# The first sixteen taps of one depthwise-conv tile move to GpSimd, and VectorE's table of filler steps is written anew

## The chip, the cores and the metric

The kernel runs on one core of a Trainium2 chip. The metric is the device time of one execution in microseconds (us); the median of three is compared. In the text PE is TensorE, DVE is VectorE, ACT is ScalarE, POOL is GpSimd, and SP is the engine that issues the DMAs.

## The reference, cut to what matters

One decoder layer over 512 positions of width 1024:

```python
h = rms_norm(x, norm_mix_g)
ca, cg, q, k, v, iq, ik, iw, z, xbc, dt = jnp.split(h @ w_in, SPLITS, axis=-1)
u = ca * jax.nn.sigmoid(cg)                  # 512 channels
u = causal_dwconv(u, conv_dw_w, conv_dw_b)   # 31 taps along the positions
u = jax.nn.silu(layer_norm(u, conv_ln_g, conv_ln_b))
att = sparse_attention(qh, kh, vh, iq, ik, iw, rel_bias)   # each query keeps its top 128 keys
y = ...                                      # Mamba-2 scan of xbc, gated by z, normed
x = x + jnp.concatenate([u, att, y], axis=-1) @ w_out
h = rms_norm(x, norm_ffn_g)
fa, fg = jnp.split(causal_dwconv(h @ w_up, ffn_conv_w, ffn_conv_b), 2, axis=-1)
x = x + (jax.nn.silu(fg) * fa) @ w_down
```

The change is about two steps. The depthwise convolution with 31 taps works on four tiles of 128 channels by 512 positions, and each tap adds a shifted copy of `u`, times one weight per channel, to a running sum. The top 128 keys are found by 16 rounds for each of three blocks of 128 queries (the first block needs none); a round takes the eight largest scores of each row and then marks them as taken.

## The kernel before, in words

All products are in split single precision: each weight chunk of 512 columns by 512 rows (or the same amount in another shape) is rounded to a high part on ACT (`w_hi`, L934), DVE subtracts it from the original for the low part (`w_lo`, L640), and PE multiplies three times. The mixing part of the layer has 23 chunks, each done in four quarters. A quarter is a slot: slot n is quarter n mod 4 of chunk n // 4, and it holds 12 matmuls of 512 columns. After its quarter, PE does small pieces of the other branches (indexer products, transposes, attention scores and so on).

One list, `PLAN`, holds all steps of the mixing part in one order, slot by slot. Every engine walks through the same list and issues its own share in that order, with semaphores between engines, so an instruction that waits holds up all that stand behind it on its engine. Within a slot come first the `front` steps (such as `logit` and `share` of the attention softmax), then the slot's matmuls and small pieces, and then the `fill` steps. The low part of chunk c is a fill step of slot 4c - 3; the high part, of slot 4c - 4.

The fill steps of DVE's long streams are set by a table, `FILL`: for each slot a string in which `1`, `2`, `3` is the next step of the top-k stream of query block 1, 2 or 3 (take the eight largest, L1357; mark them, L1362; 16 times, then the selection mask, L1367) and `a`, `d` the next tap of conv tile 0 or 3. A tap on DVE is one instruction with two SBUF inputs, `u_acc<-u_in,prm,u_acc` (L622; the first is a product alone, L617). Block 1 has 256 scores in a row, block 2 has 384, block 3 has 512.

Conv tiles 1 and 2 are on POOL, in slots that `POOL_SLOTS` names. POOL's tap is an addition of two SBUF inputs (L860); the product before it is made by ACT (`dwp`, L1129), two slots ahead, into one of four buffers named `tapped`. Product i waits until tap i - 4 is done, because it reuses its buffer. ACT stands in line behind that wait with everything else that it has: rounding the weights, evacuating the PSUM banks of q, k, v and of the indexer (`iqT` L927, `relu` L1010), the exponentials (L1052, L1060) and the evacuation of transposed probabilities (L1070).

POOL also computes the inverse roots of the q and k norms (L840), in slots 17 to 20 and 25 to 28.

An attention unit u (16 in all: four query blocks by four pairs of heads) has `score` on PE, `logit` on DVE in the next slot (L1406, which adds the bias and takes the row's minimum), the exponential on ACT, then in the slot after it the reciprocal on DVE (L1412) and the scaling on ACT (L1060), then the transpose on PE (L1773), its evacuation on ACT (L1070) and the product with v (L1975). Scores, transposes and the small products share a ring of three PSUM banks: PE can start the next one only when the bank of three before has been emptied.

The chunks are: conv 0 (slots 0 to 3), indexer (4 to 7), conv 1 (8 to 11), q, k, v (12 to 35), conv 2 and 3 (36 to 43), the scan's inputs (44 to 67), the output projection (68 to 91). After that come the feed-forward chunks, which the change does not touch.

The functions that the diff touches:

Of the kernel before, what the change touches and what calls it, by code (L numbers as in the profile page):

```python
# [20 lines left out]
CONV_CH, CONV_K = 512, 31  # L21
# [42 lines left out]
def bucket_onehot():  # L64
# [10 lines left out]

FILL = {6: "aa", 7: "aaa", 8: "aaa", 10: "1121", 11: "1212", 12: "31213", 14: "2131", 
# [4 lines left out]
        48: "ddadd", 50: "da", 51: "dd", 52: "dadd", 54: "dad", 55: "d", 56: "addda", 58: "ddd",   # L81
        59: "dd", 60: "dddd", 62: "ddd"}
POOL_SLOTS = {1: {15: 1, 16: 2, 21: 2, 22: 1, 23: 2, 24: 2, 29: 2, 30: 2, 31: 1, 32: 2, 33: 2,
# [7 lines left out]
SSD_SLOTS = (68, 72, 76, 80)  # L91
DW_POOL = (1, 2)


# [9 lines left out]
def make_plan():  # L104
# [36 lines left out]
    for j in range(4):  # L141
        streams["abcd"[j]] = iter([("dw", j, i) for i in range(CONV_K)])

# [52 lines left out]
    for j, counts in POOL_SLOTS.items():  # L196
        at_ = [n for n, k in counts.items() for _ in range(k)]
        for i, n in enumerate(at_):
            fill[n].append(("dw", j, i))
            if i:  # L200
                fill[n - 2].append(("dwp", j, i))
    for n, letters in FILL.items():
# [169 lines left out]
def build(nc, x, rel_bias, norm_mix_g, w_in, conv_dw_w, conv_dw_b, conv_ln_g, conv_ln_b, q_norm_g,  # L372
# [7 lines left out]
    with ExitStack() as ctx:  # L380
# [4 lines left out]
        def at(name, shape, dt, offset=None):  # L385

            size = (int(np.prod(shape[1:])) * (2 if dt == BF16 else 4) + 31) // 32 * 32
            if offset is None:
                offset = top[0]
                top[0] += size  # L390
            return nc.alloc_sbuf_tensor_at(name, shape, dt, offset=offset)

        def region(kb):
# [71 lines left out]
        tapped = {1: at("tapped1", [P, 4, 512], F32, r6 + 8 * K),  # L465
                  2: at("tapped2", [P, 4, 512], F32, r1)}
        gssm = at("gssm", [P, 512], F32)
        dec = at("dec", [P, SH, P], F32, rs)
# [347 lines left out]
        def _(pool):  # L816
# [25 lines left out]
            for s in PLAN:  # L842
# [5 lines left out]
                elif k == "qkms":  # L848
                    i = NT * "qk".index(s[1]) + s[2]
                    pool.wait_ge(qkms_ready, i + 1)  # L850
                    inverse_root(rqk[:, NH * i:NH * i + NH], ssqk[:, NH * i:NH * i + NH], rqk_ready)
                elif k == "dw" and s[1] in DW_POOL:

                    _, j, i = s
                    if i == 0:
                        tap(pool, j, i)
                    else:
                        pool.wait_ge(dw_taps[j], i)
                        pool.wait_ge(dwp_ready, DW_POOL.index(j) * (CONV_K - 1) + i)
                        pool.tensor_tensor(u_acc[:, j, i:], tapped[j][:, i % 4, 0:SEQ - i],  # L860
                                           u_acc[:, j, i:], ALU.add).then_inc(dw_taps[j], 1)
# [50 lines left out]
        def _(act):  # L912
# [36 lines left out]
            for s in PLAN:  # L949
# [171 lines left out]
                elif k == "dwp":  # L1121
# [3 lines left out]
                    if i > 4:  # L1125
                        act.wait_ge(dw_taps[j], i - 3)
                    elif i == 1:
                        act.wait_ge(glu_ready, j + 1)
                    act.activation(tapped[j][:, i % 4, 0:SEQ - i], u_in[:, j, 0:SEQ - i], ACT.Copy,  # L1129
                                   scale=prm[:, c:c + 1]).then_inc(dwp_ready, 1)  # L1130
# [112 lines left out]
        def _(dve):  # L1243
# [18 lines left out]
            for s in PLAN:  # L1262
# [63 lines left out]
                elif k == "glu":  # L1326
# [4 lines left out]
                        .then_inc(glu_ready, 1)  # L1331
                elif k == "dw" and s[1] not in DW_POOL:
                    tap(dve, *s[1:])
# [825 lines left out]
```

## Time and profile before

| what | value |
|---|---|
| median of 3 runs | 717.45 us (717.26 to 717.74) |
| the profiled execution's own time | 717.7 us |
| its span | 716.0 us |
| PE busy | 697.0 us, 97% of the span |
| DVE busy | 545.4 us, 76% |
| ACT busy | 380.6 us, 53% |
| POOL busy | 141.8 us, 20% |
| granted TensorE clock | 1.00 of full speed |

The profile is one execution. A row of the timeline has the start, the duration of the row, the engine, the line of the program, the operation, output and inputs, and xN for N instructions in one row; in brackets stands how long the engine had been idle before and what ended it. A PE matmul of 512 columns is shown as 0.39 us because matmuls overlap; one starts every 0.23 us.

### The profile page before, as it was taken

How to read it: one execution, taken by the hardware profiler on the slowest of the kernel's cores; microseconds unless marked ns; L12 is line 12 of the kernel's file. 1: busy time of each engine (PE TensorE's matmuls, PEld its weight loads, DVE VectorE, ACT ScalarE, POOL GpSimd, SP SyncE). 2: the span in 40 equal slices, each digit the busy share in tenths (PEclk: the TensorE clock that was granted, in tenths of full speed). 3: DMA queues.
4: the chain of work that ended last, by engine and by line, in shares of the span. 5: the costliest groups of instructions: out<-in, count | busy, mean ns of one | idle time of the engine just before them, and what ended most of it. 6: DMA issues, size and time to landing. Idle time of an engine off the chain costs nothing.

```text
span 716.0 us, 9787 instructions
## 1 busy us (share of the span) xinstructions
PE 697.0 (97%) x3402; PEld 560.4 (78%) x3402; DVE 545.4 (76%) x852; ACT 380.6 (53%) x570; POOL 141.8 (20%) x114
## 2 busy tenths in 40 slices
PE   4999999999999999999999999999999999999998
PEld 4776888667666788788888888888888888888886
DVE  4368989988898947667667777876766866997895
ACT  6254655988878765633464343343343343654660
POOL 2000477944564402233410000000000000000000
PEclk9999999999999999999999999999999999999999
DMA  8731314211111141312234588656687547864552
GB/s 245 235 127 60 118 59 117 62 60 59 59 60 60 59 177 61 135 70 60 59 118 140 173 246 249 190 170 200 186 249 237 179 160 298 297 221 140 169 162 88
DMA packets 87554, 104.09 MB, mean 145 GB/s; under 512 B 6871, under 2 KB 65591, under 8 KB 87519
## 3 DMA queue, kind: packets, MB, share of 16 engines
q1 hardware_dynamic: 87375, 103.12, 45.9%
q10 hardware_dynamic: 144, 0.52, 0.2%
q8 instruction: 20, 0.33, 0.2%
q14 instruction: 15, 0.12, 0.1%
HBM read 87.10 MB, written 16.54 MB: 145 GB/s over the span
## 4 chain that ended last, share of the span: by engine, by line
PE 87%; ACT 7%; DVE 4%; issue 2%; DMA 1%; POOL 0%; DVEq 0%; ACTq 0%
PE bank L1767 75%; PE bank L1773 4%; PE bank L1787 2%; ACT tapped L1129 1%; ACT w_hi L934 1%; PE bank L1975 1%; DVE u_acc L622 1%; PE bank L2031 1%; PE bank L1951 1%; DVE xbcT L1427 1%; PE bank L1926 1%; DMA x_in<-in_x 1%; ACT prob L1052 1%; ACT dec L1099 0%; DVE prob L1406 0%
## 5 line engine op out<-in xcount | busy, mean ns | idle before, releaser
L1767 PE MATMUL bank<-h_hi,w_hi 128*128 128x512 f32 (+1 forms) x496 | 192.9, 389 | 0.0
L1767 PE MATMUL bank<-h_lo,w_hi 128*128 128x512 f32 (+1 forms) x496 | 189.9, 383 | 0.0
L1767 PE MATMUL bank<-h_hi,w_lo 128*128 128x512 f32 (+1 forms) x496 | 189.8, 383 | 0.0
L1767 PEld LDWEIGHTS bank<-h_hi,w_hi 128*128 128x128 f32 x496 | 93.2, 188 | 25.7 <-issue 7.8
L1621 DVE SCALAR_TENSOR_TENSOR f<-bank,prm,f 128x511 f32<-128x511 f32 x88 | 65.8, 748 | 60.7 <-ACT f L1182 55.2
L1767 PEld LDWEIGHTS bank<-h_hi,w_lo 128*128 128x128 f32 x496 | 93.2, 188 | 18.4
L1767 PEld LDWEIGHTS bank<-h_lo,w_hi 128*128 128x128 f32 x496 | 93.3, 188 | 17.3
L860 POOL TENSOR_TENSOR u_acc<-tapped,u_acc 128x511 f32<-128x511 f32 (+29 forms) x60 | 90.1, 1502 | 46.1 <-ACT tapped L1129 43.0
L1182 ACT ACTIVATE f<-bank,prm 128x512 f32<-128x512 f32 x44 | 34.2, 777 | 70.4 <-PE bank L1767 70.2
L640 DVE TENSOR_TENSOR w_lo<-w_raw,w_hi 128x2048 fp32r<-128x2048 f32 x24 | 55.6, 2316 | 8.9 <-ACT w_hi L934 8.7
L1767 PE MATMUL bank<-w_hi,g_parts 128*128 128x512 f32 x168 | 53.8, 389 | 0.0
L1596 DVE TENSOR_TENSOR w_lo<-w_raw,w_hi 128x2048 fp32r<-128x2048 f32 x22 | 50.3, 2287 | 3.4 <-ACT w_hi L1171 3.4
L622 DVE SCALAR_TENSOR_TENSOR u_acc<-u_in,prm,u_acc 128x511 f32<-128x511 f32 (+29 forms) x60 | 51.9, 877 | 0.8
L1189 ACT ACTIVATE sg<-f 128x512 f32<-128x512 f32 x22 | 13.9, 632 | 72.4 <-DVE f L1621 72.4
L1129 ACT ACTIVATE tapped<-u_in,prm 128x511 f32<-128x511 f32 (+29 forms) x60 | 40.2, 704 | 21.4 <-POOL u_acc L860 15.5
L1767 PE MATMUL bank<-w_hi,h_hi 128*128 128x512 f32 x128 | 51.2, 400 | 0.0
L1767 PE MATMUL bank<-w_hi,h_lo 128*128 128x512 f32 x128 | 50.0, 390 | 0.0
L1767 PE MATMUL bank<-w_lo,h_hi 128*128 128x512 f32 x128 | 49.9, 390 | 0.0
L934 ACT ACTIVATE w_hi<-w_raw 128x2048 fp32r<-128x2048 f32 x24 | 45.8, 1910 | 3.5 <-DMA w_raw<-in_w_in 2.2
L840 POOL TENSOR_TENSOR stats<-stats 128x1 f32<-128x1 f32 (+1 forms) x24 | 23.1, 966 | 103.4 <-DVE stats L1507 35.1
L1171 ACT ACTIVATE w_hi<-w_raw 128x2048 fp32r<-128x2048 f32 x22 | 41.9, 1906 | 0.0
L1767 PEld LDWEIGHTS bank<-w_hi,g_parts 128*128 128x128 f32 x168 | 31.5, 188 | 6.6
(279 smaller groups left out, 1228.2 us busy)
## 6 DMA issues: line engine op xcount, KB each, us to landing
w_raw<-in_w_up SPq DMA_DIRECT2D x44, 512.0 KB, 6.1
w_raw<-in_w_in SPq DMA_DIRECT2D x34, 512.0 KB, 4.6
down_raw<-in_w_down SPq DMA_DIRECT2D x22, 512.0 KB, 5.4
weight_sums<-down_raw SPq DMA_DIRECT2D x11, 768.0 KB, 5.3
w_raw<-in_w_out SPq DMA_DIRECT2D x12, 512.0 KB, 4.5
weight_sums<-w_sum SPq DMA_DIRECT2D x11, 512.0 KB, 2.7
w_raw<-weight_sums SPq DMA_DIRECT2D x6, 768.0 KB, 6.0
down_raw<-weight_sums SPq DMA_DIRECT2D x5, 768.0 KB, 4.4
```

The source lines that it names most:

```text
L622: eng.scalar_tensor_tensor(out=u_acc[:, j, i:], in0=u_in[:, j, 0:SEQ - i], scalar=w, in1=u_acc[:, j, i:], op0=ALU.mult, op1=ALU.add).then_ ...
L640: eng.tensor_tensor(wlo[:, slot, cols], wraw[:, slot, cols], whi[:, slot, cols].bitcast(F32), ALU.subtract).then_inc(ready, 1)
L840: pool.tensor_tensor(out_, in_, half_neg[:, 0:n], ALU.pow).then_inc(ready, 1)
L860: pool.tensor_tensor(u_acc[:, j, i:], tapped[j][:, i % 4, 0:SEQ - i], u_acc[:, j, i:], ALU.add).then_inc(dw_taps[j], 1)
L934: act.activation(whi[:, c % NSLOT, :], wraw[:, c % NSLOT, :], ACT.Copy)\
L1129: act.activation(tapped[j][:, i % 4, 0:SEQ - i], u_in[:, j, 0:SEQ - i], ACT.Copy, scale=prm[:, c:c + 1]).then_inc(dwp_ready, 1)
L1171: act.activation(whi[:, c % NSLOT, :], wraw[:, c % NSLOT, :], ACT.Copy)\
L1182: act.activation(fbuf[:, 2 * s + v, :], bank[FFN_BANK[2 * s + v]][:, :], ACT.Identity, bias=prm[:, bass.ds(tile + R_FB, 1)], scale=prm[:, ...
L1596: dve.tensor_tensor(wlo[:, c % NSLOT, :], wraw[:, c % NSLOT, :], whi[:, c % NSLOT, :].bitcast(F32), ALU.subtract)\
L1621: ins = dve.scalar_tensor_tensor(out=fbuf[:, 2 * s + v, i:], in0=bank[FFN_BANK[2 * s + v]][:, 0:SEQ - i], scalar=prm[:, bass.ds(tile + (R_ ...
L1767: ins = pe.matmul(o, a, b, start=first and i == 0 and q == 0, stop=last and i == n - 1 and q == 2)
L1773: return pe.transpose(o, in_, ident[0:n, 0:n])
```

## The change

Tile 0's taps 0 to 15 go from DVE to POOL, in slots 6 to 14, with ACT making products 1 to 15 for them. Tile 0 shares the four `tapped` buffers of tile 1, so ACT's first product of tile 1 now waits until all 16 taps of tile 0 are done. Taps 16 to 30 of tile 0 stay on DVE, and the order of DVE's fill steps is another from slot 6 on. A product is no longer placed ahead of the slot in which its tile's first tap stands.

```diff
-FILL = {6: "aa", 7: "aaa", 8: "aaa", 10: "1121", 11: "1212", 12: "31213", 14: "2131", 
...
-        48: "ddadd", 50: "da", 51: "dd", 52: "dadd", 54: "dad", 55: "d", 56: "addda", 58: "ddd", 
-        59: "dd", 60: "dddd", 62: "ddd"}
-POOL_SLOTS = {1: {15: 1, 16: 2, 21: 2, 22: 1, 23: 2, 24: 2, 29: 2, 30: 2, 31: 1, 32: 2, 33: 2,
+FILL = {10: "11211", 11: "2121", 12: "32131", 14: "2132", 15: "12312", 16: "131a2", 18: "31", 
...
+        55: "d", 56: "dddd", 58: "ddd", 59: "d"}
+POOL_SLOTS = {0: {6: 1, 7: 2, 8: 2, 9: 2, 10: 2, 11: 2, 12: 2, 13: 1, 14: 2},
+              1: {15: 1, 16: 2, 21: 2, 22: 1, 23: 2, 24: 2, 29: 2, 30: 2, 31: 1, 32: 2, 33: 2,
...
+POOL0 = 16
+def on_pool(j, i):
+    return j in DW_POOL or (j == 0 and i < POOL0)
+def products_to(j, i):
+    return i if j == 0 else POOL0 - 1 + DW_POOL.index(j) * (CONV_K - 1) + i
...
-        streams["abcd"[j]] = iter([("dw", j, i) for i in range(CONV_K)])
+        streams["abcd"[j]] = iter([("dw", j, i) for i in range(CONV_K) if not on_pool(j, i)])
...
-                fill[n - 2].append(("dwp", j, i))
+                fill[max(n - 2, at_[0])].append(("dwp", j, i))
...
+        tapped[0] = tapped[1]
...
-                        pool.wait_ge(dwp_ready, DW_POOL.index(j) * (CONV_K - 1) + i)
+                        pool.wait_ge(dwp_ready, products_to(j, i))
...
                     elif i == 1:
                         act.wait_ge(glu_ready, j + 1)
+                        if j == DW_POOL[0]:
+                            act.wait_ge(dw_taps[0], POOL0)
```

The first place is ACT in slots 6 to 9, behind the evacuation of the first indexer tile. Before:

```order
L991 ACTIVATE u_acc<-u_acc 128x512
L927 ACTIVATE iqT<-bank 128x512 x2
L1010 ACTIVATE relu<-bank 128x256 x4
L934 ACTIVATE w_hi<-w_raw 128x2048
L1010 ACTIVATE relu<-bank 128x384 x4
```

and now:

```order
L939 ACTIVATE iqT<-bank 128x512
L1143 ACTIVATE tapped_103<-u_in,prm 128x511
L1143 ACTIVATE tapped_103<-u_in,prm 128x510
L1143 ACTIVATE tapped_103<-u_in,prm 128x509
L1143 ACTIVATE tapped_103<-u_in,prm 128x508
L1143 ACTIVATE tapped_103<-u_in,prm 128x507
L1143 ACTIVATE tapped_103<-u_in,prm 128x506
L939 ACTIVATE iqT<-bank 128x512
L1022 ACTIVATE relu<-bank 128x256 x4
L946 ACTIVATE w_hi<-w_raw 128x2048
```

Six products now stand between the evacuations of the two indexer tiles, and the last two of them wait for POOL's taps 1 and 2.

The second place is DVE from the low part of chunk 9 (slot 33) to the first `logit` (slot 35), which empties a bank of the first attention score. Before:

```order
L640 TENSOR_TENSOR w_lo<-w_raw,w_hi 128x2048
L1362 MATCH_REPLACE rank<-stats,rank 128x256
L1362 MATCH_REPLACE rank<-stats,rank 128x384
L1362 MATCH_REPLACE rank<-stats,rank 128x512
L1357 MAX stats<-rank 128x8 x2
L622 SCALAR_TENSOR_TENSOR u_acc<-u_in,prm,u_acc 128x498
L1406 ISA prob,stats<-bank,tbias 128x128
```

and now:

```order
L652 TENSOR_TENSOR w_lo<-w_raw,w_hi 128x2048
L1371 MAX stats<-rank 128x8 x2
L1376 MATCH_REPLACE rank<-stats,rank 128x512
L634 SCALAR_TENSOR_TENSOR u_acc<-u_in,prm,u_acc 128x491
L1376 MATCH_REPLACE rank<-stats,rank 128x256
L1376 MATCH_REPLACE rank<-stats,rank 128x384
L1371 MAX stats<-rank 128x8
L1420 ISA prob,stats<-bank,tbias 128x128
```

One more step, a search for the eight largest of 512, stands between the low part and the first `logit`.

The third place is DVE from the `logit` of unit 8 (slot 46) to that of unit 9 (slot 48); `att_lo` is the low part of query block 1's attention output, and behind it comes unit 8's reciprocal. Before:

```order
L617 TENSOR_SCALAR u_acc<-u_in,prm 128x512
L622 SCALAR_TENSOR_TENSOR u_acc<-u_in,prm,u_acc 128x511
L622 SCALAR_TENSOR_TENSOR u_acc<-u_in,prm,u_acc 128x510
L1418 TENSOR_TENSOR att_lo<-bank,att_hi 128x4x128
L1412 RECIPROCAL stats<-stats 128x2
```

and now:

```order
L629 TENSOR_SCALAR u_acc<-u_in,prm 128x512
L634 SCALAR_TENSOR_TENSOR u_acc<-u_in,prm,u_acc 128x511
L634 SCALAR_TENSOR_TENSOR u_acc<-u_in,prm,u_acc 128x510
L634 SCALAR_TENSOR_TENSOR u_acc<-u_in,prm,u_acc 128x509
L634 SCALAR_TENSOR_TENSOR u_acc<-u_in,prm,u_acc 128x508
L1432 TENSOR_TENSOR att_lo<-bank,att_hi 128x4x128
L1426 RECIPROCAL stats<-stats 128x2
```

Two taps more stand ahead of `att_lo` and of unit 8's reciprocal. In slots 47 to 51, that is from there to the `logit` of unit 11, there were 10 taps and are now 9.

## Rows read from the trace of the kernel before

**Rows 1.** The page: busy time of each engine.
```profile
PE 697.0 (97%) x3402; PEld 560.4 (78%) x3402; DVE 545.4 (76%) x852; ACT 380.6 (53%) x570; POOL 141.8 (20%) x114
```

**Rows 2.** Waits of PE: for whom, us in total, times, longest.
```profile
PE bank L1773 <- DVE x_normed L1274: 9.7, 1, 9.7
PE bank L1773 <- ACT dec L1099: 0.8, 2, 0.5
```

**Rows 3.** Timeline of PE: the six waits between 120 and 215 us.
```profile
128.76 0.63 PE L1773 MATMUL bank<-ident,k_tok 128*128 128x128 f32 x4 [0.80 <-ACT kT L1027]
...
136.84 0.23 PE L1947 MATMUL bank<-neg_q_bf,ident_bf 128*128 128x128 bf16 x1 [0.95 <-DVE stats L1406]
...
144.52 0.44 PE L1975 MATMUL bank<-probT,v_tok 128*64 128x128 f32 x4 [0.35 <-ACT probT L1070]
...
187.13 0.52 PE L1773 MATMUL bank<-ident,prob 128*128 128x128 f32 x3 [1.03 <-ACT prob L1060]
...
195.20 0.88 PE L1975 MATMUL bank<-probT,v_tok 128*64 128x128 f32 x12 [0.33 <-ACT probT L1070]
...
212.77 0.88 PE L1975 MATMUL bank<-probT,v_tok 128*64 128x128 f32 x12 [0.53 <-ACT probT L1070]
```

**Rows 4.** Timeline of DVE in slots 5 to 13, and its next long wait.
```profile
45.07 0.69 DVE L1330 TENSOR_TENSOR u_in<-u_in,u_acc 128x512 f32<-128x512 f32 x1 [1.27 <-ACT u_acc L991]
...
48.31 3.11 DVE L622 SCALAR_TENSOR_TENSOR u_acc<-u_in,prm,u_acc 128x511 f32<-128x511 f32 x4
...
65.38 1.61 DVE L1345 SCALAR_TENSOR_TENSOR rank<-relu,stats,rank 128x512 f32<-128x512 f32 x2 [1.02 <-ACT relu L1010]
...
71.57 2.28 DVE L640 TENSOR_TENSOR w_lo<-w_raw,w_hi 128x2048 fp32r<-128x2048 f32 x1
...
106.86 0.69 DVE L1374 TENSOR_REDUCE stats<-sq 128x8 f32<-128x512 f32 x1 [3.40 <-ACT sq L1021]
```

**Rows 5.** Timeline of PE: indexer pieces of slot 8; the first matmul of slot 16.
```profile
49.42 1.93 PE L1926 MATMUL bank<-ikT,iqT 64*128 64x256 f32 x8
...
75.68 0.39 PE L1767 MATMUL bank<-w_hi,h_hi 128*128 128x512 f32 x1
```

**Rows 6.** Timeline of ACT: indexer evacuation, first products of tile 1, a wait for POOL.
```profile
46.81 0.60 ACT L927 ACTIVATE iqT<-bank 128x512 f32<-128x512 f32 x1 [1.22 <-PE bank L1767]
50.16 0.66 ACT L1010 ACTIVATE relu<-bank 128x256 f32<-128x256 f32 x2 [2.75 <-PE bank L1926]
...
74.49 1.34 ACT L1129 ACTIVATE tapped<-u_in,prm 128x511 f32<-128x511 f32 x2 [5.85 <-DVE u_in L1330]
...
122.05 0.71 ACT L1129 ACTIVATE tapped<-u_in,prm 128x498 f32<-128x498 f32 x1 [7.27 <-POOL u_acc L860]
```

**Rows 7.** Timeline of POOL: tile 1's first taps, and seven in a row.
```profile
74.56 0.77 POOL L617 TENSOR_SCALAR u_acc<-u_in,prm 128x512 f32<-128x512 f32 x1 [62.03 <-DVE u_in L1330]
75.41 2.26 POOL L860 TENSOR_TENSOR u_acc<-tapped,u_acc 128x511 f32<-128x511 f32 x2
...
91.36 12.22 POOL L860 TENSOR_TENSOR u_acc<-tapped,u_acc 128x509 f32<-128x509 f32 x7
```

**Rows 8.** Shortest, median and longest tap in ns: on POOL, then on DVE.
```profile
L860 POOL TENSOR_TENSOR u_acc<-tapped,u_acc x60: 1035/1252/4153, 75.4 to 248.6; 128x511 f32<-128x511 f32 x2, 128x510 f32<-128x510 f32 x2, 128x509 f32<-128x509 f32 x2, 128x508 f32<-128x508 f32 x2
L622 DVE SCALAR_TENSOR_TENSOR u_acc<-u_in,prm,u_acc x60: 707/736/1632, 48.3 to 253.5; 128x511 f32<-128x511 f32 x2, 128x510 f32<-128x510 f32 x2, 128x509 f32<-128x509 f32 x2, 128x508 f32<-128x508 f32 x2
```

**Rows 9.** Timeline of DVE from the low part of chunk 9 to `logit`.
```profile
131.03 2.53 DVE L640 TENSOR_TENSOR w_lo<-w_raw,w_hi 128x2048 fp32r<-128x2048 f32 x1 [1.28 <-ACT w_hi L934]
...
136.49 0.28 DVE L1406 CUSTOM_DVE_ANT_0 prob<-bank,tbias 128x128 f32<-128x128 f32 x1
...
137.31 0.68 DVE L1357 MAX8 stats<-rank 128x8 f32<-128x512 f32 x1
```

**Rows 10.** Timeline of DVE around `att_lo` of slot 47.
```profile
182.12 2.42 DVE L622 SCALAR_TENSOR_TENSOR u_acc<-u_in,prm,u_acc 128x511 f32<-128x511 f32 x2
185.57 0.69 DVE L1418 TENSOR_TENSOR att_lo<-bank,att_hi 128x512 fp32r<-128x512 f32 x1 [1.04 <-ACT att_hi L922]
```

More of the change, by code:

```diff
@@ L72, in bucket_onehot @@
     return (np.arange(NBUCKET)[:, None] == b[None, :]).astype(np.float32)
-FILL = {6: "aa", 7: "aaa", 8: "aaa", 10: "1121", 11: "1212", 12: "31213", 14: "2131",
[4 rows of a table removed]
-        48: "ddadd", 50: "da", 51: "dd", 52: "dadd", 54: "dad", 55: "d", 56: "addda", 58: "ddd",
-        59: "dd", 60: "dddd", 62: "ddd"}
-POOL_SLOTS = {1: {15: 1, 16: 2, 21: 2, 22: 1, 23: 2, 24: 2, 29: 2, 30: 2, 31: 1, 32: 2, 33: 2,
+FILL = {10: "11211", 11: "2121", 12: "32131", 14: "2132", 15: "12312", 16: "131a2", 18: "31",
[3 rows of a table added]
+        44: "aa", 46: "ddddd", 47: "d", 48: "dddd", 50: "ddd", 51: "d", 52: "ddddd", 54: "ddd",
+        55: "d", 56: "dddd", 58: "ddd", 59: "d"}
+POOL_SLOTS = {0: {6: 1, 7: 2, 8: 2, 9: 2, 10: 2, 11: 2, 12: 2, 13: 1, 14: 2},
[1 row of a table added]
                   34: 1, 35: 2, 36: 1, 37: 2, 38: 2, 39: 1, 40: 2, 41: 1},
@@ L851, in _ @@
                     inverse_root(rqk[:, NH * i:NH * i + NH], ssqk[:, NH * i:NH * i + NH], rqk_ready)
-                elif k == "dw" and s[1] in DW_POOL:
+                elif k == "dw" and on_pool(*s[1:]):
                     _, j, i = s
@@ L1331, in _ @@
                         .then_inc(glu_ready, 1)
-                elif k == "dw" and s[1] not in DW_POOL:
+                elif k == "dw" and not on_pool(*s[1:]):
                     tap(dve, *s[1:])
```

7 rows, old and new, of the table FILL are left out of this document.

## The prediction

> **What bounds the kernel now.** I read the page first. PE is busy 97% of the span, at the full clock, and DVE, the engine that the change unloads, 76% [rows 1]. So the change can win only what PE stands still. The list of PE's waits gives the largest as 9.7 us before the first norm [rows 2], which nothing here touches. The timeline of PE has six waits between 120 and 215 us: 0.80 + 0.95 + 0.35 + 1.03 + 0.33 + 0.53 = 3.99 us [rows 3]. Late in the mixing part there is 0.8 us of waiting on the scan's exponentials [rows 2], behind ACT and not behind a tap. About 4 us, 0.6% of the time, is all that the new table can give. Next I looked at whose work ends each of the six: a product or an exponential of ACT for five, DVE's first `logit` for one [rows 3].
>
> **Part by part.** The sum is made against the profiled execution, 717.7 us (span 716.0 us and 1.7 around it). The median of the runs is 717.45, 0.25 lower, and I take that off at the end.
>
> *Taps 0 to 15 leave DVE.* Eight of them stood in slots 6 to 8, at 3.11 us for four [rows 4], some 6 us. After them DVE waits 1.02 us for ACT at 65.38, and 3.40 us at 106.86 for the squares of k [rows 4]. A lead that DVE has in slot 10 is gone at these two places, since what ends them comes from PE by way of ACT. The other eight stood in slots 22 to 36, but by the letters of the two tables DVE's filler from slot 22 to slot 43 is about as heavy as before: 63 top-k steps and 14 taps then, 65 and 12 now, because top-k steps and tile 0's other taps move up into the room. So the unloading is worth 0 in the stretch where PE waits. What counts there is only which steps stand between two given instructions.
>
> *ACT and POOL in slots 6 to 14.* Now 15 products go into ACT's line, at 0.62 us from one to the next (the pair that takes 1.34 us [rows 6], of which 0.72 is the second). Tile 0's input is ready at 45.76 [rows 4]. Four products take ACT to 48.3, the fifth to 48.9. The sixth waits for POOL's tap 2. POOL's tap 0 takes 0.77 and each next one 1.13 [rows 7], so tap 2 ends at 45.9 + 0.8 + 2.3 = 49.0, and the sixth product at 49.6. Only then comes the second indexer tile's evacuation, at 50.2 instead of 47.4 [rows 6]. PE's eight indexer matmuls start at 49.42, and the fifth, the first that needs that tile, at 50.3 [rows 5]. The cost is 0.1 us; at POOL's slower pace of 12.22 / 7 = 1.75 us [rows 7] the tap ends at 50.2 and the cost is 1.3. I take 0.1, because DVE now has nothing with two SBUF inputs there. POOL's 16 taps end between 45.9 + 0.8 + 15 x 1.25 = 65 (median [rows 8]) and 45.9 + 0.8 + 15 x 1.75 = 73, before tile 1's first product at 74.49 [rows 6], so the new wait on 16 taps costs 0. Behind it would stand the high part of chunk 5 and the evacuation of q.
>
> On POOL the taps collide with DVE. A DVE tap takes 0.74 us at the median and 1.63 at the longest; one of POOL's 1.25, and 4.15 at the longest [rows 8]. In slots 8 to 11 DVE's sums of the indexer scores, also with two SBUF inputs, now run beside POOL. Those before 65.38 end in a wait. After it come three, each at most 0.9 us longer (1.63 - 0.74), so the low part of chunk 4 starts between 71.57 and 74.3 and ends 2.28 later [rows 4], and PE wants it at 75.68 [rows 5]: 0 to 0.9 us. I take 0, since most taps are at the median.
>
> The Trainium skill, SBUF — State Buffer, "SBUF: two separate sides", says that the port pair which VectorE and GpSimd share is an exclusive lock for the whole instruction. By that rule each of the three could lose a whole POOL tap (1.25 at the median), the low part would end at 77.6, and PE would lose 1.9 us. The longest DVE tap, 1.63 us, exceeds the median by less than one POOL tap, which agrees with the rule, and the median shows how seldom it bites.
>
> *Slots 22 to 32.* The wait of 0.80 us at 128.76 is ACT's, and ACT was late by its products, one of which waited 7.27 us for POOL [rows 6]. POOL's program is the same from tile 1 on, and before its inverse roots DVE has about the same steps. I take 0, with 0.5 us either way.
>
> *Slots 33 and 34.* DVE's low part of chunk 9 starts when ACT's high part is there (it waited 1.28 us) [rows 9], which does not move. Between it and the first `logit` there is one search of 512 more. It took 0.60 us from start to start (0.68 in its row [rows 9]), and PE's wait of 0.95 at 136.84 [rows 3] ends with that `logit`. So I add 0.6. Bounds: 0, if ACT's high part comes earlier by as much, and 1.5, if the tap there now hits a POOL tap (0.9 more). The `logit` is followed on ACT by the exponential, the scaling and the next evacuations, and these carry the 0.6 on to 144.52.
>
> *Slots 44 to 51.* `att_lo` began at 185.57 after an idle 1.04 us [rows 10]. Two taps more stand ahead of it, at 0.74 each, 1.48 in all: it comes 0.4 us late, or 2.2 late if both collide (0.9 each). I take 0.6. Unit 8's reciprocal is behind it, and PE's wait of 1.03 at 187.13 [rows 3] grows by that. From there to the `logit` of unit 11 DVE has one tap less, -0.7. PE's waits of 0.33 and 0.53 at 195.20 and 212.77 are paced by that chain, so they give back up to 0.7 (at most their own 0.86). Net -0.1, with bounds of -1.1 (no delay at `att_lo`, a collision less) and +1.5.
>
> *The end three slots sooner.* Tile 3's last tap stood in slot 62 and its first reader is in slot 67, with no PE wait between 213 and 270. Worth 0.
>
> Sum: 0.1 + 0 + 0 + 0.6 - 0.1 = +0.6 us, so 718.3 for the profiled execution and 718.0 for the median.
>
> **The rivals.** A: *slower by the early slots.* ACT stands behind POOL from slot 7 on and DVE's sums behind POOL's taps. For it speaks the pace of 1.75 us in one run of seven taps [rows 7]. Against it, that run was beside a DVE with weight splits and taps. It decides when tap 2 ends after about 49.1, or the low part of chunk 4 starts after 73.4. Price 1.3 for the indexer evacuation and 0.9 at slot 16: 718.0 + 2.1 = 720.1 us.
>
> B: *faster.* With fewer taps beside POOL, POOL keeps a better pace, ACT waits less in slots 29 to 33, and the 0.80 and 0.95 at 128 and 136 shrink; in slots 48 to 51 both small waits go. For it: ACT's wait of 7.27 us on POOL and the chance of fewer collisions. Against it: as many taps and steps stand in these slots as before. Worth 0.80 + 0.95 + 0.86 = 2.6 without the 0.6 of my sum: 714.8 us.
>
> C: *the lead of 6 us lives on* and all six waits go: 717.45 - 4.0 = 713.5 us. DVE's idle 3.40 us at 106.86 speaks against it.
>
> **How the numbers follow.** My forecast, within 1.4 us of before, has 0.50, A 0.27, B 0.18, C 0.05. What a measurement can tell is 0.2%, 1.4 us. Of B and C nearly all is beyond that, of A all but a little, and the forecast's upper side (collisions at two places, +0.9 and +1.6) gives some to slower: faster 0.22, same 0.49, slower 0.29. The range leaves out C, the lower half of B and A's upper end: 715.2 to 720.3. The forecast's own range is 716.6 to 719.3.
>
> **What would show it.** In the changed profile: DVE's idle at about 65 larger by some 2 to 4 us, and the one at 106.86 unchanged within 1 us; the evacuation of the second indexer tile near 50 and no wait of PE there over 0.3; POOL done with tile 0 before 73 and no wait of ACT ahead of tile 1's first product except for its input; the wait at the first `logit` near 1.5 us instead of 0.95; the wait at unit 8's transpose near 1.6; those at 195 and 212 smaller or gone. Wrong would be: PE waiting at all between 45 and 120 us (A), or six waits that sum to under 2.5 us (B, C).

## The result, and the profile after

The changed kernel takes 725.23 us (median; 722.98 to 727.24) against 717.47: a ratio of 1.0108, 95% interval 1.0091 to 1.0125. That is 7.8 us slower. The forecast was 718.0 (715.2 to 720.3), so the time lies above the whole range. The executions of one kernel, which agree within 0.5 us before, now spread over 4 us. The profiled execution took 725.24 us, span 723.2.

The page after, to set beside [rows 1]:

```profile
PE 700.6 (97%) x3398; PEld 562.9 (78%) x3402; DVE 545.5 (75%) x836; ACT 389.9 (54%) x585; POOL 158.7 (22%) x130
```

DVE has 16 instructions less and is busy exactly as long as before: 545.5 us. What it lost in taps it got back as longer instructions. The waits of PE after (for whom; us in total, times, longest), to set beside [rows 2]:

```profile
PE bank L1787 <- ACT prob L1072: 2.8, 1, 2.8
PE bank L1961 <- DVE stats L1420: 2.0, 1, 2.0
PE bank L1940 <- ACT relu L1022: 1.4, 1, 1.4
```

Three waits stand out that before were 1.03, 0.95 and nothing [rows 3]. The timeline of PE shows where they are:

```profile
50.09 0.99 PE L1940 MATMUL bank<-ikT,iqT 64*128 64x256 f32 x4 [0.24 <-issue]
56.94 0.88 PE L1940 MATMUL bank<-ikT,iqT 64*128 64x384 f32 x2 [1.43 <-ACT relu L1022]
...
131.22 0.63 PE L1787 MATMUL bank<-ident,k_tok 128*128 128x128 f32 x4 [0.55 <-ACT kT L1039]
...
140.33 0.23 PE L1961 MATMUL bank<-neg_q_bf,ident_bf 128*128 128x128 bf16 x1 [1.98 <-DVE stats L1420]
...
193.54 0.52 PE L1787 MATMUL bank<-ident,prob 128*128 128x128 f32 x3 [2.77 <-ACT prob L1072]
```

The waits account for less than half of the loss: the six waits of [rows 3] were 3.99 us together, and those of the changed kernel from 45 to 225 us are 0.24 + 1.43 + 0.55 + 1.98 + 2.77 + 0.20 = 7.17, while the span grew by 7.2. The rest is in the clock. The view by windows of the changed kernel (length, then busy time and count of PE, its weight loads, DVE, ACT and POOL, then PE's granted clock, where 0.50 is half speed throughout, then DMA share and GB/s):

```profile
58.00:60.00 2.00, 2.00 (x7) 1.57 (x7) 1.79 (x3) 1.27 (x3) 0.54 (x1) 0.63 0.04 12
60.00:62.00 2.00, 2.00 (x7) 1.49 (x5) 1.93 (x3) 0.74 (x2) 1.64 (x2) 0.52 0.01 4
62.00:64.00 2.00, 2.00 (x9) 0.87 (x8) 2.00 (x1) 0.56 (x2) 0.51 (x1) 1.00 0.00 0
...
140.00:142.00 2.00, 1.67 (x7) 1.28 (x8) 2.00 (x10) 1.69 (x6) 1.82 (x2) 0.61 0.16 48
142.00:144.00 2.00, 2.00 (x7) 1.55 (x6) 2.00 (x9) 2.00 (x7) 1.51 (x2) 0.54 0.00 0
...
194.00:196.00 2.00, 2.00 (x9) 0.99 (x7) 1.90 (x3) 1.48 (x3) 1.28 (x2) 0.76 0.00 0
196.00:198.00 2.00, 2.00 (x7) 1.52 (x6) 1.96 (x7) 1.23 (x5) 1.19 (x1) 0.50 0.00 0
```

In this execution TensorE runs some 3.4 us at half clock behind each of the three long waits (1.2 GHz instead of 2.4). PE counts as fully busy there, so the page's 97% hides it. The kernel before has no such stretch up to its end. The timeline of PE at the first one:

```profile
58.08 0.39 PE L1781 MATMUL bank<-h_lo,w_hi 128*128 128x512 f32 x1
58.31 0.45 PE L1781 MATMUL bank<-h_hi,w_lo 128*128 128x512 f32 x1
...
60.26 0.63 PE L1781 MATMUL bank<-h_lo,w_hi 128*128 128x512 f32 x1
60.69 0.63 PE L1781 MATMUL bank<-h_hi,w_lo 128*128 128x512 f32 x1
```

From 0.23 us between two starts it goes to 0.43. Eight such steps make 1.6 us.

With the start of the same matmul in both traces as the measure, the difference (after minus before) grows like this:

| PE, time before | difference | what happened since the line above |
|---|---|---|
| 16 us | -0.34 | start-up |
| 56.6 | +1.12 | waits of 0.24 and 1.43 |
| 59.6 | +2.71 | half clock, +1.59 |
| 129 | +2.46 | wait 0.55 instead of 0.80 |
| 137.0 | +3.49 | wait 1.98 instead of 0.95 |
| 140.3 | +4.98 | half clock, +1.49 |
| 144.5 | +4.57 | the wait of 0.35 is gone |
| 187.1 | +6.41 | wait 2.77 instead of 1.03 |
| 191.6 | +7.95 | half clock, +1.54 |
| 213 | +7.24 | waits of 0.33 and 0.53 now 0 and 0.20 |

From there on it stays, up to the difference of the spans, 7.2 us. Waits added 4.2 us, the half clock 4.6, and 1.4 was given back where a later wait absorbed lateness; 0.3 was won at the start.

**Who is late at 56.94.** The timelines of DVE and POOL in the changed kernel from 46 us, where DVE's small steps for the time steps of the scan (`dt`) stand beside POOL's taps:

```profile
46.44 0.19 DVE L1326 TENSOR_TENSOR stats<-stats 128x32 f32<-128x32 f32 x1
46.66 0.96 DVE L1327 SCALAR_TENSOR_TENSOR stats<-stats 128x32 f32<-128x32 f32 x1
47.66 1.13 DVE L1329 TENSOR_TENSOR stats<-stats 128x32 f32<-128x32 f32 x1
...
49.06 1.14 DVE L1333 SCALAR_TENSOR_TENSOR stats<-stats 128x32 f32<-128x32 f32 x1
50.30 1.34 DVE L1355 TENSOR_SCALAR rank<-relu,stats 128x256 f32<-128x256 f32 x1
51.75 2.99 DVE L1359 SCALAR_TENSOR_TENSOR rank<-relu,stats,rank 128x256 f32<-128x256 f32 x3
...
61.54 3.12 DVE L652 TENSOR_TENSOR w_lo<-w_raw,w_hi 128x2048 fp32r<-128x2048 f32 x1
...
75.09 2.28 DVE L652 TENSOR_TENSOR w_lo<-w_raw,w_hi 128x2048 fp32r<-128x2048 f32 x1
```

```profile
46.44 7.43 POOL L872 TENSOR_TENSOR u_acc<-tapped,u_acc 128x511 f32<-128x511 f32 x6
55.95 2.59 POOL L872 TENSOR_TENSOR u_acc<-tapped,u_acc 128x505 f32<-128x505 f32 x2 [2.08 <-ACT tapped L1143]
```

A step over 32 columns takes 0.96 to 1.14 us in place of 0.19, which is about the rest of POOL's 1.24 us tap. The first step of the indexer's sum, a TENSOR_SCALAR that reads one tensor from SBUF and not two, takes 1.34, where the same shape took 0.35 before, and the three behind it 2.99 for 1.66. The low part of chunk 4 starts at 75.09, 3.5 us later than in [rows 4]. Between them the searches (MAX8) and markings, which are most of DVE's filler, keep their 0.4 to 0.7 us. This agrees with the Trainium skill, SBUF — State Buffer, "SBUF: two separate sides": of a VectorE instruction with two SBUF inputs and a GpSimd instruction that reads SBUF, whichever comes second is blocked until the other ends. Not every step is hit: in the same rows some of 32 columns still take 0.19.

### The profile page after: what moved, and what is told of

The parts are those of the page before. It is cut to its first block, busy times and chain, and to the rows that moved or that the text cites. A ratio compares the mean times of both kernels' runs of the same rounds, so it can differ in the third digit from the quotient of the medians.

```text
span 723.2 us, 9814 instructions
## 1 busy us (share of the span) xinstructions
PE 700.6 (97%) x3398; PEld 562.9 (78%) x3402; DVE 545.5 (75%) x836; ACT 389.9 (54%) x585; POOL 158.7 (22%) x130
## 4 chain that ended last, share of the span: by engine, by line
PE 83%; ACT 6%; DVE 5%; issue 3%; POOL 2%; DMA 1%; ACTq 0%; DVEq 0%; POOLq 0%
PE bank L1781 72%; PE bank L1787 3%; ACT w_hi L946 2%; PE bank L1801 2%; PE bank L1965 1%; POOL u_acc L872 1%; PE bank L1989 1%; DVE u_acc L634 1%; PE bank L2045 1%; DVE rank L1376 1%; DMA x_in<-in_x 1%; DVE w_lo L652 1%; ACT tapped L1143 1%; PE bank L1961 0%; POOL stats L852 0%
## 5 line engine op out<-in xcount | busy, mean ns | idle before, releaser
L1781 PE MATMUL bank<-h_hi,w_hi 128*128 128x512 f32 (+1 forms) x496 | 194.9, 393 | 0.0
L872 POOL TENSOR_TENSOR u_acc<-tapped,u_acc 128x510 f32<-128x510 f32 (+22 forms) x75 | 106.3, 1417 | 63.9 <-ACT tapped L1143 60.1
L652 DVE TENSOR_TENSOR w_lo<-w_raw,w_hi 128x2048 fp32r<-128x2048 f32 x24 | 57.3, 2388 | 9.2 <-ACT w_hi L946 9.2
L1143 ACT ACTIVATE tapped<-u_in,prm 128x510 f32<-128x510 f32 (+22 forms) x75 | 49.9, 704 | 20.2 <-POOL u_acc L872 15.1
L1610 DVE TENSOR_TENSOR w_lo<-w_raw,w_hi 128x2048 fp32r<-128x2048 f32 x22 | 50.3, 2286 | 3.4 <-ACT w_hi L1185 3.4
L634 DVE SCALAR_TENSOR_TENSOR u_acc<-u_in,prm,u_acc 128x496 f32<-128x496 f32 (+29 forms) x45 | 41.7, 927 | 0.8
```

Of the source, the lines that this page charges most:

```text
L634: eng.scalar_tensor_tensor(out=u_acc[:, j, i:], in0=u_in[:, j, 0:SEQ - i], scalar=w, in1=u_acc[:, j, i:], op0=ALU.mult, op1=ALU.add).then_ ...
L652: eng.tensor_tensor(wlo[:, slot, cols], wraw[:, slot, cols], whi[:, slot, cols].bitcast(F32), ALU.subtract).then_inc(ready, 1)
L1610: dve.tensor_tensor(wlo[:, c % NSLOT, :], wraw[:, c % NSLOT, :], whi[:, c % NSLOT, :].bitcast(F32), ALU.subtract)\
L1781: ins = pe.matmul(o, a, b, start=first and i == 0 and q == 0, stop=last and i == n - 1 and q == 2)
```

## The experiments

Theory: three places (the early collisions, slot 34, slot 46) make PE wait, and a longer wait brings the half clock. Rivals: ACT's longer line of products makes the early wait; the late waits are only the early lateness passed on; the half clock comes from the added work of POOL.

**Only the offload, with the old table.**

```
-FILL = (the new table)
+FILL = (the old table without its first 16 letters "a"; POOL_SLOTS[0] stays)
```

> Taps 0 to 15 of tile 0 are on GpSimd as in the changed kernel, but VectorE keeps the old table, from which only those 16 letters a are removed. My theory: the changed kernel loses 7.7 us in three separate places, each a PE wait that grew (1.43, 1.98, 2.77 us) and each followed by 3.41 us at the half clock, which costs some 1.6 us. The first place belongs to the offload and stays: wait of 1.4 us near 57, one stretch at half clock, +2.5 to +3. The second and third belong to the new order (one step more ahead of the first logit, two taps more ahead of att_lo) and go: waits under 1.1 us there, clock full. Time 718.5 to 720.5. Rival 1 (the early delay of ACT and GpSimd is what makes the later waits): all three stay, 724 to 726. Rival 2 (the order alone, the offload costs nothing): 716.5 to 717.5.

719.17 us (718.86 to 719.50), ratio 1.0024 [1.0015, 1.0034]. The timeline of PE up to 80 us:

```profile
56.85 0.88 PE L1935 MATMUL bank<-ikT,iqT 64*128 64x384 f32 x2 [1.36 <-ACT relu L1017]
78.47 0.50 PE L1776 MATMUL bank<-w_hi,h_hi 128*128 128x512 f32 x1 [1.59 <-DVE w_lo L647]
```

Here the profiled execution kept the full clock, and the next wait is for the low part of chunk 4. At 100 us PE is 2.92 late, in the changed kernel 2.72. So the half clock at 58 us cost nothing more: without it PE meets the late low part and waits. The time is inside the expected range, but the half clock that was part of that sum is not in this trace. Later this kernel wins: eight taps less in slots 22 to 36, no wait at the first `logit`, and the lateness is 0.60 us at 137 and 0.9 at the end.

**Only the table: nothing on POOL early.**

```
-  pool.tensor_tensor(u_acc[:, 0, i:], tapped[0][...], u_acc[:, 0, i:], ALU.add)
+  pool.tensor_scalar(u_acc[:, 0, 0:8], u_in[:, 0, 0:8], 1.0, None, ALU.mult)
-  fill[...].append(("dwp", 0, i))        # no products of tile 0 on ACT
```

Taps 0 to 15 of tile 0 are left out.

> The changed kernel without the work of taps 0 to 15 of tile 0: GpSimd does 16 short operations on 8 columns in their place and ACT makes no products for them. The table is the new one. My theory: the wait near 57 and its stretch at half clock go, the other two stay: 725.2 - 3 = 722 us, two stretches at half clock. Rival 1: all three go, 717 to 718. Rival 2: nothing changes, 725.

719.88 us (719.03 to 721.25), 1.0038 [1.0025, 1.0050]. PE is early by 0.35 us at 100 us and its two late waits are there all the same:

```profile
137.28 0.23 PE L1965 MATMUL bank<-neg_q_bf,ident_bf 128*128 128x128 bf16 x1 [1.95 <-DVE stats L1424]
...
188.83 0.52 PE L1791 MATMUL bank<-ident,prob 128*128 128x128 f32 x3 [2.32 <-ACT prob L1076]
```

So they belong to the table and are not passed on. The time is 2 us under the 722 that was expected: the trace has neither of the two half-clock stretches that belonged to that sum. Executions with a mean granted clock of 1.000 took 719.03 to 719.52, two with 0.997 and 0.998 took 720.24 and 720.28, one with 0.995 took 721.25: by these clocks the same program has no, one or two half-clock stretches, at about 1 us each.

By the medians the offload alone costs 1.8 us and the table alone 2.5, together 7.8. The 3.5 us that are left belong to neither alone. Two things in the traces account for them in part: the old table let the early lateness shrink from 2.92 to 0.60 us, which the new one does not, and the changed kernel's trace has three half-clock stretches where these two have none.

**Products without additions, and additions without products.**

```
 e7:  POOL's 16 operations on tile 0 cut to 8 columns; ACT's products whole
 e8:  ACT's 15 products cut to 8 columns; POOL adds u_in, whole
```

Both leave out part of tile 0's convolution.

> The changed kernel with the 15 products of tile 0 still made on ACT in full, but GpSimd's 16 operations on tile 0 cut to 8 columns. It tells ACT's longer line from the collisions of GpSimd with VectorE. If the collisions make the early wait (VectorE's small steps took 0.96 to 1.14 us instead of 0.19 beside GpSimd's taps), the wait near 57 goes: VectorE's short steps back at 0.19, wait under 0.4, 722 us as without the taps. If ACT's line alone makes it (1.31 us of products ahead of the relu that frees the bank), a wait of 0.5 to 1.3 us stays, under the length that takes the clock down or near it: 722.5 to 725.

> The changed kernel with GpSimd's 16 taps of tile 0 in full size (reading u_in in place of the product) and ACT's 15 products cut to 8 columns. If the collisions alone make the early wait, it stays near 1.4 us with its stretch at half clock: 725. If both are needed (my guess: the relu comes 0.8 us late by the collisions and 1.3 by the products), a wait of 0.2 to 0.8 us stays, the clock stays full: 722.5 us.

e7: 721.11 us (720.18 to 722.10), 1.0053 [1.0039, 1.0067]. e8: 726.02 us (724.96 to 726.39), 1.0122 [1.0107, 1.0138]. With the products alone PE doesn't wait before 128 us and is 0.14 early at 100, and DVE's small steps take 0.19 us, as before. With the additions alone PE is 2.94 late at 100, as in the changed kernel (2.72). The wait near 57 is 0.60 in that kernel, as guessed if both were needed, but the time is that of the whole loss and not 722.5. The timelines of PE and DVE of e8:

```profile
55.94 0.88 PE L1943 MATMUL bank<-ikT,iqT 64*128 64x384 f32 x2 [0.60 <-ACT relu L1024]
78.47 0.50 PE L1784 MATMUL bank<-w_hi,h_hi 128*128 128x512 f32 x1 [2.49 <-DVE w_lo L652]
```

```profile
46.50 0.96 DVE L1330 SCALAR_TENSOR_TENSOR stats<-stats 128x32 f32<-128x32 f32 x1
...
47.73 0.97 DVE L1333 SCALAR_TENSOR_TENSOR stats<-stats 128x32 f32<-128x32 f32 x1
48.73 1.30 DVE L1336 SCALAR_TENSOR_TENSOR stats<-stats 128x32 f32<-128x32 f32 x1
```

The early loss is POOL's additions beside DVE. ACT's line only decides where it surfaces, at 57 or at 78 us.

The run with the products alone shows one thing more. A line each from DVE's timeline, from PE's and from the view by windows:

```profile
47.06 0.19 DVE L1335 TENSOR_TENSOR stats<-stats 128x32 f32<-128x32 f32 x1
```

```profile
189.69 0.52 PE L1793 MATMUL bank<-ident,prob 128*128 128x128 f32 x3 [2.77 <-ACT prob L1078]
```

```profile
190.00:192.00 2.00, 2.00 (x11) 1.04 (x10) 1.90 (x3) 1.63 (x4) 1.12 (x2) 1.00 0.00 0
```

PE waits 2.00 us at 137 and 2.77 at 189, as long as in the changed kernel at the same two matmuls, and the clock stays full behind both. The length of the wait does not decide alone.

**One tap behind the logit.**

```
-FILL 34: "a123", 35: "123"
+FILL 34: "123",  35: "a123"
```

> The changed kernel with one letter of its table moved: the tap of slot 34 stands in slot 35, behind the first logit. Theory L (late places in the table): the wait of 1.98 us before the first score transposes falls to about 1 us or below, since one tap that took 1.40 us leaves the stretch between ACT's high part of chunk 9 and the first logit; with it goes the half-clock stretch behind that wait. 0.9 to 2.5 us are won on 725.2, so 722.7 to 724.3. Rival (the wait is DVE's accumulated lateness from the collisions in slots 6 to 16): the wait keeps 1.9 us, the time stays at 725.2 +- 0.4.

723.52 us (722.23 to 724.03), 1.0085 [1.0072, 1.0099]. The wait falls from 1.98 to 0.66, as expected. The wait of 2.75 at 191.67 stays, and in this trace the clock behind it is full.

**Two taps of slot 46 later.**

```
-FILL 46: "ddddd", 54: "ddd"
+FILL 46: "ddd",   54: "ddddd"
```

> The changed kernel with two of the five taps of slot 46 moved to slot 54, behind unit 8's att_lo and the chain to unit 11. Theory L: PE's wait at unit 8's probability transpose falls from 2.77 us to about 1.0 (what it was before the change: 1.03), since the last two taps, at 1.22 us each, stand between the end of slot 45 and att_lo; a half-clock stretch behind it goes too. 1.7 to 3.2 us are won on 725.2, so 722.0 to 723.5. Rival (att_lo is late because ACT is late, not for the taps): att_lo then waits for ACT, the wait keeps over 2 us, and the time falls by less than 0.7.

723.19 us (723.02 to 724.58), 1.0090 [1.0076, 1.0104]. The wait at unit 8 falls from 2.77 to 1.44, less than expected, and new waits of 0.47 and 0.91 stand at 226 and 236 us, behind the two taps' new place. The half clock behind unit 8 is gone in this trace, and so is the one behind the first `logit`, whose wait is still 1.99.

**All three edits; both moves of the table.** Here the third edit sets tile 0's products one slot ahead of their tap instead of two.

```
-                fill[max(n - 2, at_[0])].append(("dwp", j, i))
+                fill[max(n - (2 if j else 1), at_[0])].append(("dwp", j, i))
```

> The changed kernel with both moves of the table together (slot 34's tap behind the logit, two taps of slot 46 in slot 54), and tile 0's products one slot ahead of their tap instead of two, so that ACT meets POOL's pace later. Theory: what remains is the early part. Waits at 140 and 193 at or below 1.0 us, the wait of 1.43 near 57 us stays (the run in which ACT made the products and POOL added nothing had no wait there, so the products' places aren't its cause): 719 to 721.5. If the products' places count after all, the wait near 57 falls below 0.7 and the time comes to 717.5 to 718.7.

> The changed kernel with both moves of the table (slot 34's tap behind the logit, two taps of slot 46 in slot 54) and tile 0's products where the changed kernel has them. Each move alone gave 723.5 and 723.2 against 725.2, and all three edits together 724.7. If the two moves add and it was the third edit (products one slot ahead) that lost, since it only moved PE's wait from 57 us to the low part of chunk 4 at 79, this run comes to 721.0 to 722.3, with a wait of 1.4 near 57 and none near 79. Rival: the moves cost each other, and the time is 723 to 725 without the third edit too.

All three: 724.68 us (723.13 to 724.80), 1.0096 [1.0080, 1.0111]. Both moves alone: 722.88 us (722.60 to 723.00), 1.0077 [1.0063, 1.0091]. Both came out above what was expected, and the two moves do not add: alone they won 1.7 and 2.0 us, together 2.4. The traces of the first move and of both have one half-clock stretch each, behind the wait near 57, so they compare without the clock: the second move wins 1.4 us up to 213 us and pays 1.5 between there and 250. What it won by itself goes with the half clock that is missing there. The third edit did lower the wait at 57 us, from 1.4 to 0.73, and paid 2.47 for it at 78.73, with the half clock behind that wait (by windows, as above):

```profile
80.00:82.00 2.00, 2.00 (x6) 1.52 (x6) 2.00 (x8) 2.00 (x3) 1.84 (x3) 0.50 0.87 305
```

At 100 us this kernel is 4.79 late, the one without the third edit 2.80. A half-clock stretch at 58 us lies ahead of the late low part and is absorbed. The executions say the same: both moves alone gave 723.00 twice at a mean clock of 1.000 and 722.60 to 722.88 at 0.997; all three gave 723.13 at 1.000 and 724.59 to 724.80 at 0.997 and 0.998.

**POOL starts later.**

```
-POOL0 = 16;  POOL_SLOTS 0: {6: 1, 7: 2, 8: 2, 9: 2, 10: 2, 11: 2, 12: 2, 13: 1, 14: 2}
+POOL0 = 12;  POOL_SLOTS 0: {9: 2, 10: 2, 11: 2, 12: 2, 13: 2, 14: 2}
 (one "a" more in each of slots 18, 19, 20, 23 and 25, one less in 16; the moves of slots 34 and 46)
```

> Both moves of the table as in the run of all three, and POOL starts tile 0 in slot 9 instead of slot 6 and takes 12 taps instead of 16 (four more stay on VectorE, in slots 18 to 25). Collision theory: the two-input steps of DVE up to the second mask (until 58 us) run alone, so the step of 0.19 us stays 0.19 and PE doesn't wait before 60 us; the low part of chunk 4 is late by at most 2 us. 716.5 to 718.5. Rival (ACT's longer line makes the early wait, whoever adds): ACT's 11 products still stand between evacuations, a wait of 1 us or more appears between 57 and 80 us, and the time is 719 to 721.

724.17 us (723.59 to 724.32), 1.0094 [1.0079, 1.0109]. Half of the mechanism came out as expected: the steps before 58 us run alone, and nothing waits before 60 us. The low part of chunk 4 was to be late by at most 2 us and starts 3.9 later than in [rows 4]. The rival foretold a wait between 57 and 80 us too, and one is there, but it is for DVE's low part and not for ACT. The taps now stand beside the indexer's last sums and a weight split. DVE's timeline:

```profile
46.59 0.19 DVE L1322 SCALAR_TENSOR_TENSOR stats<-stats 128x32 f32<-128x32 f32 x1
...
58.04 1.11 DVE L1359 TENSOR_TENSOR rank<-rank,neg_q 128x128 f32<-128x128 f32 x1
59.18 3.13 DVE L647 TENSOR_TENSOR w_lo<-w_raw,w_hi 128x2048 fp32r<-128x2048 f32 x1
62.24 1.49 DVE L1350 TENSOR_SCALAR rank<-relu,stats 128x512 f32<-128x512 f32 x1
```

The low part of chunk 4 ends as late as ever, PE waits 2.33 for it, and the half clock behind it has nothing left to absorb it: 3.86 at 100 us.

**The kernel before, with the filler of slots 24 to 35 rearranged.** Two tries for a kernel faster than both.

```
 e10: FILL of before, 34: "12a" -> "12",  35: "1321" -> "1321a"
 e11: FILL of before, 24: "2a13121" -> "2a13121a", 25: "3" -> "3aa",
      31: "23a12" -> "2312", 32: "3121a3" -> "31213", 34: "12a" -> "12"
```

> The kernel before (all taps of tile 0 on VectorE), with slot 34's tap moved to slot 35, behind the first logit. If the logit's place in the row sets PE's wait there, the wait of 0.95 near 137 falls by 0.7 and a wait at the next product of ACT grows by some of it: 716.6 to 717.2. If ACT's exponentials behind it pace PE anyway, the time stays at 717.4 +- 0.2.

> The kernel before with the taps of slots 31, 32 and 34 moved to slots 24 and 25, ahead of DVE's idle 3.40 us at 106.86. The run with the old table and tile 0's first 16 taps on POOL lacked these taps too, and PE's shift fell there from +2.92 at 100 us to +0.60 at 137. Theory (room in slots 28 to 34 is worth what PE waits at 128 and 136): both waits, 0.80 + 0.95, go or shrink, and the time is 715.4 to 716.8, below both kernels. Rival (ACT's products that wait for POOL pace slots 28 to 33): only the logit's 0.7 is won, 716.6 to 717.3.

e10: 718.04 us (717.96 to 718.29), 1.0010 [1.0001, 1.0019]. e11: 718.46 us (718.28 to 718.81), 1.0016 [1.0007, 1.0025]. Both expectations failed, and in the wrong direction. In e10 the wait at the `logit` fell from 0.95 to 0.26, and the tap, now between the first `logit` and its reciprocal, took 1.59 us in place of 0.71. ACT then waited for the reciprocal, and PE for ACT:

```profile
135.88 0.23 PE L1941 MATMUL bank<-neg_q_bf,ident_bf 128*128 128x128 bf16 x1 [0.26 <-DVE stats L1400]
140.26 0.53 PE L1767 MATMUL bank<-ident,prob 128*128 128x128 f32 x2 [0.79 <-ACT prob L1054]
144.97 0.44 PE L1969 MATMUL bank<-probT,v_tok 128*64 128x128 f32 x4 [0.70 <-ACT probT L1064]
```

In e11 the taps brought forward made the low part of a later chunk late (0.77 at 121), and the wait of 0.70 at 145 appears there too. No kernel tried beats the one before.

**A long wait alone.** The kernel before, with three taps brought to slot 34, ahead of the first `logit`.

```
-FILL 34: "12a",    36: "32a2", 38: "a232", 39: "3a232"
+FILL 34: "12aaaa", 36: "322",  38: "232",  39: "3232"
```

> The kernel before with three more taps in slot 34, ahead of the first logit (from slots 36, 38 and 39). It asks whether a longer wait of PE alone, with none of the change, brings a stretch at half clock. PE's wait near 137 grows from 0.95 to about 3.1 (three taps at 0.73). If such a wait can do it: a stretch at half clock behind it in at least some of the executions, and 719.5 to 721.5 with differences of 1 us and more between executions. If it needs what the change brought (POOL beside DVE in slots 6 to 14): clock 1.0 in every execution and 719.0 to 719.8.

723.25 us (722.84 to 724.10), 1.0086 [1.0072, 1.0100]. The four taps took 5.22 us (1.3 each, not 0.73), PE waits 5.42, and the half clock follows, in all five executions (mean clock 0.995 each). By windows:

```profile
138.00:140.00 2.00, 0.00 (x0) 0.00 (x0) 1.96 (x2) 0.00 (x0) 1.92 (x2) 0.58 0.00 1
140.00:142.00 2.00, 1.00 (x6) 0.66 (x6) 2.00 (x8) 1.02 (x5) 0.21 (x1) 0.50 0.00 0
...
144.00:146.00 2.00, 2.00 (x8) 1.57 (x7) 1.19 (x5) 2.00 (x7) 1.55 (x2) 0.71 0.00 0
```

Nothing of the change is in this kernel. A wait of 5.42 us is enough for the half clock; the rival that asks for POOL's added work falls. That waits of 2.0 to 2.8 us can do it without POOL's early additions is seen only in the mean clocks of the two runs that lack them (down to 0.995), not in a trace. The time is above the expected 719.5 to 721.5, because the wait is.

## Why the prediction was wrong, step by step

*What bounds the kernel.* Right for what could be won: only waits of PE. For what could be lost I priced a wait of PE at its length. In the profiled execution those of 1.43, 1.98 and 2.77 us also brought the half clock, some 1.5 us each that PE counts as busy. This term is missing in the sum. At the first place it took the room of a wait for the low part of chunk 4 (1.59 us without it), so it is a loss of its own at the other two.

*ACT and POOL in slots 6 to 14.* The step that failed most. The second indexer tile was evacuated at 49.41 (predicted near 50), and PE waited 0.24 there. The wait came at the score matmuls of query block 2 (384 columns) instead, for a bank that `relu` empties. "I take 0.1, because DVE now has nothing with two SBUF inputs there" is wrong. DVE had the small steps of `dt`, the sums and a weight split there. I counted only the three sums behind the idle of 1.02 us at 65, since "those before 65.38 end in a wait". That idle was no cover: what ended it was PE's indexer matmul by way of ACT, and ACT's evacuations wait for DVE's sums themselves, as the timeline of ACT in the changed kernel shows:

```profile
51.73 0.38 ACT L1022 ACTIVATE relu<-bank 128x256 f32<-128x256 f32 x1 [1.19 <-DVE rank L1355]
53.02 0.38 ACT L1022 ACTIVATE relu<-bank 128x256 f32<-128x256 f32 x1 [0.91 <-DVE rank L1359]
```

So the chain of evacuation and sum was late as a whole. Two of my signs failed with it: DVE's idle at 65 us was to grow by 2 to 4 us and is gone, and the one of 3.40 at 106.86 was to stay within 1 us and fell to 1.31. Predicted for this part: +0.1. Measured: in the changed kernel, with the old table and with the additions alone PE is 2.7 to 2.9 late at 100 us, without the additions 0.1 to 0.4 early, so about 3 us are theirs. POOL was done with tile 0 at 74.6, not before 73, and tile 1's first product did not wait for it, as predicted. The lock rule of the Trainium skill, weighed at 1.9 us in the prediction, was nearer than the median I took; it was set on too few instructions.

*Slots 22 to 32.* Predicted 0. The wait at 128.76 fell from 0.80 to 0.55 (-0.25). Right.

*Slots 33 and 34.* Predicted +0.6 with a bound of +1.5. Measured +1.0, in the changed kernel (0.95 to 1.98) and with the table alone (0.95 to 1.95): the search is the 0.6, and the tap there took 1.40 instead of 0.71, less 0.24 that the low part of chunk 9 was shorter. The size was inside its bounds, the choice of the lower one wrong. The timeline of DVE, to set beside [rows 9]:

```profile
133.49 2.29 DVE L652 TENSOR_TENSOR w_lo<-w_raw,w_hi 128x2048 fp32r<-128x2048 f32 x1 [1.30 <-ACT w_hi L946]
...
137.15 1.40 DVE L634 SCALAR_TENSOR_TENSOR u_acc<-u_in,prm,u_acc 128x491 f32<-128x491 f32 x1
...
140.00 0.27 DVE L1420 CUSTOM_DVE_ANT_0 prob<-bank,tbias 128x128 f32<-128x128 f32 x1
```

*Slots 44 to 51.* Predicted +0.6 at `att_lo` and -0.7 given back. Measured +1.7 at unit 8's transpose and -0.7 given back (0.33 and 0.53 became 0 and 0.20). To set beside [rows 10]:

```profile
187.17 4.90 DVE L634 SCALAR_TENSOR_TENSOR u_acc<-u_in,prm,u_acc 128x511 f32<-128x511 f32 x4
191.99 0.68 DVE L1432 TENSOR_TENSOR att_lo<-bank,att_hi 128x512 fp32r<-128x512 f32 x1
```

`att_lo` no longer waits for ACT. A tap takes 1.22 here: two of them are 2.45 and not 1.48, and less the idle of 1.04 that makes 1.4. Moving the two away (2.77 to 1.44) confirms it. The price stood in my own rows: the two taps ahead of `att_lo` took 2.42 us in [rows 10], and I charged 0.74 each. The giving back was right.

*One error behind three steps.* The median of 0.74 us [rows 8] is that of all 60 taps, most of which stand where POOL is idle. In the trace of the kernel before, 39 of them overlap no tap of POOL and take 0.71 to 0.75 us; the 20 that overlap one by more than 0.1 us take 0.71 to 1.63, with a median of 1.25. At the places that counted it was 1.22, 1.40, 1.30 and 1.59. I took the collision for the upper bound; it is the ordinary case there.

*The end three slots sooner.* Worth 0, as predicted: the difference is constant from 213 us on.

*The rivals.* A named the right place and sign ("PE waiting at all between 45 and 120") and had the right mechanism as one of its two parts: DVE's sums behind POOL's taps, priced at 0.9 where they cost about 3. ACT's longer line, priced at 1.3, cost nothing by itself. The late waits and the clock were in neither. B's idea, that fewer taps on DVE in slots 22 to 36 shrink the waits at 128 and 136, holds with the old table (both gone, though PE came there 2.9 late, which shrinks such waits too); the new one fills that room again. Room made by moving taps won nothing in the two rearranged kernels; fewer taps there without the early lateness were not tried. C was out.

*What adds up.* The profiled execution: -0.3 start, +1.46 and +1.59 early, -0.25, +1.03 at the logit, +1.49 clock, -0.4, +1.74 at unit 8, +1.54 clock, -0.7. What stays open is when a wait brings the half clock. A wait of 1.36 at 57 us did in one kernel and did not in another; 1.59 and 2.49 at 78.47 did not, 2.47 at 78.73 did; 1.98 and 2.77 did in the changed kernel, and 2.00 and 2.77 at the same matmuls did not with the products alone.

## What to carry to other kernels

Before work is moved to GpSimd, list every VectorE instruction with two SBUF inputs that will then run beside it, the tiny ones too, and TENSOR_SCALAR from SBUF to SBUF (1.34 us for 0.35 here), and charge each one up to the rest of a GpSimd instruction; a median over the whole kernel is no price for an instruction whose neighbours are known. An engine's idle time is no cover if what ends it comes back through the engine itself. On a TensorE that is 97% busy, a wait can cost more than it grows: 0.95 to 1.98 us cost 2.5 here, and 1.03 to 2.77 cost 3.3. A wait further on can take some of it back: read the granted clock in windows of a few microseconds, since the busy share shows nothing of it.

## What the runs showed of the hardware

A half-clock stretch of 3.4 us stood behind some waits of PE of 1.35 to 2.8 us and not behind others as long, with matmuls of 512 columns at 0.43 us instead of 0.23; it lasted about twice that around a wait of 5.42. The same program has it in some executions and not in others (with the table alone 719.1, 720.3 and 721.25 us with mean clocks of 1.000, 0.998 and 0.995), so a kernel with such waits also spreads. That is only part of the 4 us here against 0.5 before: 722.98 us had a mean clock of 0.997, but 725.2 and 727.24 both had 0.993, and what parts those two is open. VectorE steps over 32 columns with two SBUF inputs take up to 1.30 us beside a GpSimd addition, instead of 0.19; MAX8 and MATCH_REPLACE8 over 256 columns take 0.42 and 0.41 us with GpSimd adding or idle.
